# Sliding attention: the third of the bias table that repeats, loaded from DRAM in place of copied by GpSimd

## What is computed

```
dist = qi + SWA_BLOCK - ki                      # qi in 0..127, ki in 0..255
bias = rel_table[t5_bucket(dist)]               # one value for each of 16 heads
s = einsum('bnqhgd,bnkhd->bnhgqk', q, kb) + bias
s = where((dist >= 0) & (dist < 128) & (key_pos >= 0), s, NEG_INF)
m = maximum(max(s), sink);  p = exp(s - m)
probs = p / (sum(p) + exp(sink - m))
```

## Time and profile before

| | us |
|---|---|
| median of 3 runs | 1292.92 |
| the runs | 1297.89, 1292.92, 1292.64 |
| the profiled execution | 1305.34 |
| its span in the trace | 1303.5 |
| PE busy of that span | 1263.1 (97%) |
| POOL busy | 239.2 (18%) |

### The profile page before, as it was taken

How to read it: one execution, slowest core, us unless ns; L and a number is a source line. 1 busy time by engine, 2 the same in 40 slices (tenths; PEclk the granted TensorE clock), 3 DMA queues, 4 the chain that set the end, 5 groups by cost and what they waited for, 6 DMA issues and landing times.

```text
span 1303.5 us, 28434 instructions
## 1 busy us (share of the span) xinstructions
PE 1263.1 (97%) x10440; PEld 1228.4 (94%) x10440; DVE 912.6 (70%) x1643; ACT 769.8 (59%) x1282; POOL 239.2 (18%) x221
## 2 busy tenths in 40 slices
PE   7999999999999999987998999999999999999997
PEld 7999999988999999987898989999999889999997
DVE  5866557976787665798686256777766697777754
ACT  5544445696554444658854386666665466766642
POOL 0000000010000000035376010154430120355400
PEclk9999999999999999999999599999999999999999
DMA  7655564563366656544477024666587633666563
GB/s 226 209 171 166 146 176 153 175 205 87 114 195 191 180 155 189 165 158 179 118 223 191 2 64 131 195 192 190 174 196 194 197 98 113 181 186 183 153 190 109
DMA packets 87740, 212.53 MB, mean 163 GB/s; under 512 B 19365, under 2 KB 34021, under 8 KB 87536
## 3 DMA queue, kind: packets, MB, share of 16 engines
q1 hardware_dynamic: 85440, 204.58, 52.5%
q0 software_dynamic: 1664, 6.48, 2.1%
q10 hardware_dynamic: 560, 0.44, 0.1%
HBM read 208.41 MB, written 3.06 MB: 162 GB/s over the span
## 4 chain that ended last, share of the span: by engine, by line
PE 83%; DVE 7%; ACT 4%; DMA 3%; issue 2%; SPq 1%; DVEq 0%; ACTq 0%
PE bank L531 20%; PE bank L533 20%; PE bank L532 20%; PE bank L2819 2%; PE bank L2821 2%; PE bank L2820 2%; DVE wl L399 1%; PE bank L1632 1%; ACT wh L394 1%; PE bank L1634 1%; PE bank L1633 1%; DVE dQK L2341 1%; PE bank L508 1%; PE bank L504 1%; PE bank L2920 1%
## 5 line engine op out<-in xcount | busy, mean ns | idle before, releaser
L394 ACT ACTIVATE wh<-raw 128x1024 fp32r<-128x1024 f32 (+3 forms) x423 | 407.7, 970 | 350.9 <-PE bank L533 288.3
L399 DVE TENSOR_TENSOR wl<-raw,wh 128x1024 fp32r<-128x1024 f32 (+3 forms) x369 | 406.1, 1104 | 150.8 <-ACT wh L394 149.9
L531 PE MATMUL bank<-XH,wh 128*128 128x256 f32 (+1 forms) x1448 | 410.8, 284 | 2.9 <-DVE XL L971 2.7
L533 PE MATMUL bank<-XH,wl 128*128 128x256 f32 (+1 forms) x1448 | 410.2, 283 | 0.0
L532 PE MATMUL bank<-XL,wh 128*128 128x256 f32 (+1 forms) x1448 | 409.9, 283 | 0.0
L531 PEld LDWEIGHTS bank<-XH,wh 128*128 128x128 f32 x1448 | 273.4, 189 | 3.9 <-DVE XL L971 3.1
L533 PEld LDWEIGHTS bank<-XH,wl 128*128 128x128 f32 x1448 | 273.7, 189 | 0.0
L532 PEld LDWEIGHTS bank<-XL,wh 128*128 128x128 f32 x1448 | 272.2, 188 | 0.0
L531 PE MATMUL bank<-AH,wh 128*128 128x256 f32 (+1 forms) x704 | 198.6, 282 | 0.0
L533 PE MATMUL bank<-AH,wl 128*128 128x256 f32 (+1 forms) x704 | 198.5, 282 | 0.0
L532 PE MATMUL bank<-AL,wh 128*128 128x256 f32 (+1 forms) x704 | 198.2, 282 | 0.0
(11 more groups left out here) (391 smaller groups left out, 2253.1 us busy)
## 6 DMA issues: line engine op xcount, KB each, us to landing
raw<-in_w_up SPq DMA_DIRECT2D x175, 512.0 KB, 4.0
raw<-in_w_down SPq DMA_DIRECT2D x64, 384.0 KB, 3.4
raw<-in_w_down SPq DMA_DIRECT2D x64, 320.0 KB, 3.4
raw<-in_w_gvz SPq DMA_DIRECT2D x32, 512.0 KB, 4.1
raw<-in_w_gqk SPq DMA_DIRECT2D x16, 512.0 KB, 4.8
raw<-in_w_gout SPq DMA_DIRECT2D x16, 512.0 KB, 4.5
raw<-in_w_mv SPq DMA_DIRECT2D x8, 512.0 KB, 4.7
raw<-in_w_mqk SPq DMA_DIRECT2D x8, 512.0 KB, 4.7
```

The costliest lines, as they stand in the source:

```text
L394: eng.activation(WH[s][:, 0:n, :], raw[s][:, 0:n, :], ACT.Copy).then_inc(s_hi[s], 1)
L399: eng.tensor_tensor(WL[s][:, 0:n, :], raw[s][:, 0:n, :], WH[s][:, 0:n, :].bitcast(F32), ALU.subtract).then_inc(s_lo[s], 1)
L531: eng.matmul(out, WH[s][:, i, :], xh, start=start, stop=False)
L533: mm = eng.matmul(out, WL[s][:, i, :], xh, start=False, stop=stop)
```

## The change

`load_bias` issues a second transfer behind each of the eight: columns 0 to 127 of the same 16 partitions x 16 heads, 256 pieces of 512 bytes (128 KB), read from the same values of `bias_d` as columns 256 to 383. The four copies are gone from GpSimd's order, and `b(h)` waits for the semaphore of the loads at 256, which is sixteen transfers, in place of the copy.

```diff
                     src = bass.AP(tensor=bias_d.tensor, offset=P - 1 - p0, ap=[[3 * P - 1, 16], [3 * P * 16, 16], [1, 2 * P]])
                     eng.dma_start(BT[p0:p0 + 16, :, P:3 * P], src).then_inc(self.mb, 16)
+                    src = bass.AP(tensor=bias_d.tensor, offset=2 * P - 1 - p0, ap=[[3 * P - 1, 16], [3 * P * 16, 16], [1, P]])
+                    eng.dma_start(BT[p0:p0 + 16, :, 0:P], src).then_inc(self.mb, 16)
...
-                    "dup0 snk0 snk1 snk2 snk3 dup1 snk4 dup2 snk5 dup3 snk6 snk7 snk8 snk9 snk11 snk13 snk10"
+                    "snk0 snk1 snk2 snk3 snk4 snk5 snk6 snk7 snk8 snk9 snk11 snk13 snk10"
...
                     eng.wait_ge(*T.past(f"s{h}"))
-                    eng.wait_ge(*G.past(f"dup{h // 4}"))
+                    eng.wait_ge(self.kv.mb, 256)
...
-                def dup(kv):
-                    eng.wait_ge(self.kv.mb, 128)
-                    G.done(eng.tensor_copy(BT[:, 4 * kv:4 * kv + 4, 0:P], BT[:, 4 * kv:4 * kv + 4, 2 * P:3 * P]), f"dup{kv}")
```

More of the change, by code:

```diff
@@ L3361, in snk @@
                     G.done(eng.tensor_copy(sb[:, 3 * P + 1:3 * P + 2], v("sink", h)), f"snk{h}")
-                dup(0)
                 snk(0)
@@ L3367, in pool @@
                 snk(3)
-                dup(1)
                 snk(4)
-                dup(2)
                 snk(5)
-                dup(3)
                 snk(6)
```

## The result

| | median us | lowest to highest |
|---|---|---|
| before, 20 runs | 1298.01 | 1288.51 to 1307.75 |
| changed, 20 runs | 1303.45 | 1296.64 to 1317.24 |

The ratio is 1.0075, with a 95% interval of 1.005 to 1.010. On 1298 us that is +9.7 us, between +6.5 and +13. The two medians lie only 5.4 us apart and the two means 7.2: before's executions fall into two groups, nine from 1288.5 to 1293.4 and eleven from 1297.9 to 1307.8, and its median stands in the second. The forecast was +2.4 with bounds of +0.4 to +6.4, and a time of 1291.5 to 1299.3. It was wrong: the direction was right and the size much too small. The rival that dragged the weights, +10.4 us, has the right size, and whether it has the right mechanism is what the experiments are about.

What follows compares the result with a forecast made beforehand. TensorE, busy 97% of the span, was taken to bound the kernel, waiting on skv's third weight tile. The sum -0.6 + 0 + 0 + 1.0 + 2.0 = +2.4 us on 1292.92 gave 1295.3 us, range 1291.5 to 1299.3.

Steps and rivals of the forecast that it cites:

- The rival that dragged the weights: Weight packets stand behind bias loads on the same engines, 3.0 us per added transfer: +10.4 us, 1303.3; chance beyond +6.5: 0.07.
- the issues on GpSimd: Eight more transfers issued by GpSimd, 0.58 us each, 4.7 us in all, fit into its idle time: cost nothing.
- The 0.6 us of the copies: End of down3: without two copies beside them, VectorE's wl and XL on the chain get shorter, -0.6 us (bounds 0 to -0.6).
- Part 3, the price: One added transfer holds all DMA engines for 1.0 us, half an old bias load's 2.0 us; upper bound 2.0 us.
- Such a limit goes by bytes: The 16-partition destination, not the piece, makes a bias load dear, so half the bytes cost half: 1.0 us.
- Part 4, the start of down3: Added loads at end of up3 and start of down3 delay a down3 weight tile: +1.0 us (bounds 0 to +3.0).
- Four, of which the last two matter: Of four added transfers around down3's start, only two count: 2.0 us of transfers less 1.0 of slack, +1.0 us.
- Part 4, before skv: Two added transfers ahead of skv's third weight tile, with zero slack, delay TensorE: +2.0 us (bounds +1.0 to +4.0).

Runs made afterwards that it cites:

- e7_all8_copies: Kernel before, four copies kept, second transfer added at all eight bias loads; first bias load to first b 219.1 us (before 207.4), ratio 1.0056.
- e4_stride_before: Kernel before with each bias load on 16 partitions at a stride of 8 instead of neighbouring ones; first bias load to first b 206.4 us, ratio 0.9970.
- e5_stride_after: Changed kernel with all sixteen transfers on partitions at a stride of 8; first bias load to first b 207.3 us (changed kernel 219.4), ratio 0.9962.
- e2_ends: Kernel before, copies kept, second transfer only at start of up3 and end of down3 (n = 0, 1, 6, 7); first bias load to b 213.4 us, ratio 1.0066.
- e1_mid: Kernel before, copies kept, second transfer only at end of up3 and start of down3 (n = 2 to 5); first bias load to b 212.9 us, ratio 1.0014.
- e9_only45: Kernel before, copies kept, second transfer only at the two bias loads of down3's first iteration; first bias load to first b 211.3 us, ratio 1.0040.
- e6_warm_after: Changed kernel with 18 and 14 unread filler matmuls in TensorE's waits at down3's start and for XL; first bias load to b 214.3 us, ratio 1.0014.

## Why the prediction was wrong

- **The frame was right.** The copies and the new wait in `b` are off the path (19 us early), and the issues on GpSimd cost nothing visible. The 0.6 us of the copies is in the instructions, and `e7_all8_copies` shows that it doesn't reach the total.
- **Part 3, the price: mis-sized.** 1.0 us forecast, 1.33 measured, because of the neighbouring partitions (`e4_stride_before`, `e5_stride_after`). "Such a limit goes by bytes" failed where it was used: half the bytes of an old load cost on average 0.83 of its time (1.33 against 1.61). It was 0.9 as the mean of the two ends (`e2_ends`) and 1.5 around the start of down3 (`e1_mid`), where the transfers come closest together. One price taken from one load before skv was used for all.
- **Part 4, the start of down3: the step that failed.** "Four, of which the last two matter" gave +1.0 us; measured are waits of 4.9 us, and of 3.7 in `e1_mid` and `e7_all8_copies`. In after the four pairs there go out from 937.95 to 951.90 us, and they form one pile: the weights of down3 issued from 947 to 954 us take 10.8 to 11.6 us to land, where those of before around the same loads took 3.9 to 6.4. One of them is the tile that TensorE waits for. For two transfers alone the step would nearly have held (1.6 us in `e9_only45`).
- **Part 4, before skv: right in kind, too small.** Forecast 9 to 10 us for the load and a wait for `XL` of 2.9 us; measured 9.96 and 3.5. That it came so near is in part luck: with the copies kept the same sum gives 3.5 us, and 5.0 (`e2_ends`) and 5.2 (`e7_all8_copies`) were measured.
- **The clock: no term at all.** The sum took every us of waiting as one us of time. Each of the two waits was followed by a stretch at 1.2 GHz, 4.2 us together by the ledger and about 5 by `e6_warm_after`, some four tenths of the loss. Rows of before could have led there: a wait of 3.7 us in an earlier stage, and the four us behind it at a clock of 0.58. The prediction used only its windows around skv, all at 1.00.

```profile
577.76 0.55 PE L2819 MATMUL bank<-XH,wh 128*128 128x256 f32 x1 [3.72 <-DVE dZ L1057]
```
```profile
577.00:581.00 4.00, 3.24 (x15) 3.27 (x16) 3.93 (x8) 1.42 (x2) 1.51 (x1) 0.58 0.60 227
```

- **The rival with +10.4 us had the right size and about half of the mechanism.** Weights held back while bias loads are in flight are what the changed kernel shows (81 GB/s at 955 us), but its waits grew by 6.9 us in all, not by 10.4; most of the rest is the clock, so the match in size is in part luck. It had a chance of 0.07, and the reason given against it, half the bytes and so half the slow stretch, is contradicted by 1.33 us for an added transfer where a whole old load took 1.6.

## What to carry to other kernels

Count every transfer that reaches the engines within one load's time of a critical tile as one pile, not only the last ones in front of it. A wait of TensorE of some us can cost more than itself: here 3.5 to 4.9 us of waiting brought another 1.6 to 2.6 us of slow matmuls. And before small loads are made cheaper, look whether they can stand elsewhere: the same loads where the weights had slack made TensorE wait for nothing, in each of the three forms tried.

## What the hardware showed beyond that

- 16 partitions at a stride of 8 took 0.59 of the DMA time of 16 neighbouring ones, for the same bytes and pieces (3.6 against 6.1 us for each MB).
- Pieces of 256 bytes to 16 partitions were no dearer by the byte than pieces of 512: 0.70 us for 64 KB, 1.33 us for 128 KB. Both are dearer by the byte than the old loads of 1 KB pieces (1.61 us for 256 KB); the runs don't tell whether that is the piece or the crowding.
- Equal waits at one place don't have equal sequels. TensorE waited 2.25 us in before and 2.21 us in `e4_stride_before` for the same tile of an earlier stage (`dQK`), and the next four us ran at a clock of 1.00 and of 0.57:

```profile
595.00:599.00 4.00, 3.50 (x24) 2.99 (x25) 3.86 (x8) 3.63 (x8) 0.78 (x2) 1.00 0.27 87
```
```profile
594.00:598.00 4.00, 4.00 (x23) 3.97 (x24) 3.86 (x8) 3.62 (x7) 1.19 (x2) 0.57 0.29 82
```

- One execution can spend some 37 us at half clock (before, 0.51 from 710 to 747 us) in a stage that the next runs at full clock (1.00 in after from 700 to 800 us), so that two profiled totals differ by more than the change does.
